# Attention units on one core: the value products issued ahead of the transposes, while score products still come

## The reference, cut to what matters

```python
s = q @ k.T                       # scores; 2nd attention adds a window mask, 4th a position bias
p = softmax(s)                    # 2nd: with one extra "sink" logit in the denominator
o = p @ v
```

## Time and profile before

| | us |
|---|---|
| median of 3 executions | 2563.8 (2560.21 to 2565.89) |
| the profiled execution's own time | 2560.08 |
| span of the profiled execution | 2558.3 |

### The profile page before, as it was taken

How to read it: one execution, slowest core, us unless ns; L and a number is a source line. 1 busy time by engine, 2 the same in 40 slices (tenths; PEclk the granted TensorE clock), 3 DMA queues, 4 the chain that set the end, 5 groups by cost and what they waited for, 6 DMA issues and landing times.

```text
span 2558.3 us, 46168 instructions
## 1 busy us (share of the span) xinstructions
PE 2429.6 (95%) x17946; PEld 1976.9 (77%) x17946; DVE 1678.2 (66%) x2767; ACT 1057.3 (41%) x1748; POOL 375.1 (15%) x340
## 2 busy tenths in 40 slices
PE   7999999989898999999999999889999999899987
PEld 4888888857776788888788888779997875577866
DVE  3777787665555787788877754675555325666665
ACT  4222234365344522222522223555455344555354
POOL 2000011023353200000100001001013700120052
PEclk9999999999999999999999999999999999999999
DMA  7655663200000365566455542324563221023301
GB/s 269 232 192 195 194 204 114 89 23 3 3 4 24 118 208 194 192 195 203 165 195 191 193 142 84 101 75 160 184 175 107 91 95 50 1 66 132 124 18 50
DMA packets 88422, 323.35 MB, mean 126 GB/s; under 512 B 9712, under 2 KB 10864, under 8 KB 87504
## 3 DMA queue, kind: packets, MB, share of 16 engines
q1 hardware_dynamic: 86864, 310.68, 37.3%
q0 software_dynamic: 1408, 10.59, 1.1%
HBM read 320.18 MB, written 1.05 MB: 126 GB/s over the span
## 4 chain that ended last, share of the span: by engine, by line
PE 82%; DVE 9%; ACT 3%; issue 3%; DVEq 1%; DMA 1%; POOL 0%; POOLq 0%; ACTq 0%; SPq 0%
PE bank L503 22%; PE bank L504 22%; PE bank L505 22%; PE bank L1397 1%; DVE row_statistics L1451 1%; PE bank L1406 1%; PE bank L2239 1%; DVE weights_hi_lo L409 1%; PE bank L1422 1%; PE bank L2245 1%; DMA weight_ring<-stream_k 1%; PE bank L1824 1%; ACT weights_hi_lo L404 1%; PE bank L2876 1%; DVE work L3226 1%
## 5 line engine op out<-in xcount | busy, mean ns | idle before, releaser
L404 ACT ACTIVATE weights_hi_lo<-weight_ring 128x1024 fp32r<-128x1024 f32 (+1 forms) x379 | 394.7, 1041 | 1082.3 <-PE bank L505 1057.0
L503 PE MATMUL bank<-input_hi,weights_hi_lo 128*128 128x512 f32 (+1 forms) x2032 | 743.0, 366 | 15.9 <-DVE weights_hi_lo L409 9.8
L409 DVE TENSOR_TENSOR weights_hi_lo<-weight_ring,weights_hi_lo 128x1024 fp32r<-128x1024 f32 (+1 forms) x373 | 453.1, 1215 | 436.9 <-ACT weights_hi_lo L404 435.4
L504 PE MATMUL bank<-input_lo,weights_hi_lo 128*128 128x512 f32 (+1 forms) x2032 | 739.4, 364 | 0.0
L505 PE MATMUL bank<-input_hi,weights_hi_lo 128*128 128x512 f32 (+1 forms) x2032 | 739.4, 364 | 0.0
L503 PEld LDWEIGHTS bank<-input_hi,weights_hi_lo 128*128 128x128 f32 x2032 | 385.7, 190 | 82.9 <-issue 19.8
L504 PEld LDWEIGHTS bank<-input_lo,weights_hi_lo 128*128 128x128 f32 x2032 | 385.7, 190 | 60.5 <-issue 0.7
L505 PEld LDWEIGHTS bank<-input_hi,weights_hi_lo 128*128 128x128 f32 x2032 | 385.4, 190 | 59.7
L503 PE MATMUL bank<-hidden_hi_lo,weights_hi_lo 128*128 128x512 f32 (+1 forms) x936 | 335.6, 359 | 1.4 <-DVE hidden_hi_lo L1111 1.1
L504 PE MATMUL bank<-hidden_hi_lo,weights_hi_lo 128*128 128x512 f32 (+1 forms) x936 | 333.6, 356 | 0.0
L505 PE MATMUL bank<-hidden_hi_lo,weights_hi_lo 128*128 128x512 f32 (+1 forms) x936 | 333.6, 356 | 0.0
(11 more groups left out here) (525 smaller groups left out, 2967.1 us busy)
## 6 DMA issues: line engine op xcount, KB each, us to landing
weight_ring<-stream_k SPq DMA_DIRECT2D x498, 512.0 KB, 3.5
weight_ring<-stream_f SPq DMA_DIRECT2D x64, 448.0 KB, 3.4
weight_ring<-stream_f SPq DMA_DIRECT2D x32, 512.0 KB, 3.7
extra_tiles<-condrows POOLq DMA_DIRECT2D x3, 1024.0 KB, 9.1
constants<-consts POOLq DMA_DIRECT2D x1, 2112.5 KB, 9.4
residual_stream<-xin SPq DMA_DIRECT2D x1, 2048.0 KB, 11.3
work<-nabias POOLq DMA_DIRECT2D x1, 2048.0 KB, 9.4
residual_stream<-ctx POOLq DMA_DIRECT2D x1, 1024.0 KB, 6.0
```

Of the source, the lines that this page charges most:

```text
L404: act.activation(split_place(place)[:, 0, 0:words], w[:, 0:words], ACT.Copy).then_inc(hi_ready, 1)
L409: eng.tensor_tensor(split_place(place)[:, 1, 0:words], ring[:, n % RING, 0:words], split_place(place)[:, 0, 0:words].bitcast(F32), ALU.sub ...
L503: pe.matmul(out, weights[:, 0, w], x_hi, start=first, stop=False)
L504: pe.matmul(out, weights[:, 0, w], x_lo, start=False, stop=False)
```

## The change

In iterations that still issue scores (`it < n`), TensorE multiplies M(it-3) before it transposes T(it-2). In the last three iterations the old order stays. Transposes and value products move unchanged into two helper functions, `turn` and `mix`, with all their waits; instructions, operands and the other engines' programs are the same.

```diff
@@ -1375,6 +1375,34 @@
                 pe.wait_ge(rope_spread, 8)
             if which == "na":
                 pe.wait_ge(heads_ready, a + 1)
+            def turn(u):
+                pe.wait_ge(probs_scaled, u0 + u + 1)
+                if u >= 1:
+                    pe.wait_ge(turned_copied, u0 + u)
+                for b in range(2):
+                    for i in range(len(key_tiles(which, pairs[u][1]))):
+                        mm = pe.transpose(pb[4 + b][:, tok(i)], attention_probs(which, u)[:, b, tok(i)], C("ident"))
+                mm.then_inc(probs_turned, 1)
+
+            def mix(u):
+                t, qt = pairs[u]
+                keys = key_tiles(which, qt)
+                if which == "odd" and u == n - 1:
+                    odd_out_half(pe, 0, range(6))
+                pe.wait_ge(turned_copied, u0 + u + 1)
+                if which == "odd" and u >= 1:
+                    pe.wait_ge(mixed_copied, u0 + u)
+                elif u >= 2:
+                    pe.wait_ge(mixed_copied, u0 + u - 1)
+                for i, tile in enumerate(keys):
+                    for b in range(2):
+                        ch = attention_operands(which, t, b, qt)[2]
+                        mm = pe.matmul(mix_bank(which, u)[HD * b:HD * b + HD, 0:P], attention_values(which, tile, ch),
+                                       attention_turned(which, u)[:, b, tok(i)], start=i == 0, stop=i == len(keys) - 1)
+                mm.then_inc(mixed, 1)
+                if which == "odd" and u == n - 1:
+                    odd_out_half(pe, 1, range(KT - 1))
+
             for it in range(n + 3):
                 if which == "even" and it == 0:
                     pe.wait_ge(qk_normed, 5)
@@ -1396,34 +1424,12 @@
                         q, k, _ = attention_operands(which, t, b, qt)
                         mm = pe.matmul(pb[2 * (it % 2) + b][:, 0:nk], q, k[:, 0:nk], start=True, stop=True)
                     mm.then_inc(scores_ready, 1)
-                u = it - 2
-                if 0 <= u < n:
-                    pe.wait_ge(probs_scaled, u0 + u + 1)
-                    if u >= 1:
-                        pe.wait_ge(turned_copied, u0 + u)
-                    for b in range(2):
-                        for i in range(len(key_tiles(which, pairs[u][1]))):
-                            mm = pe.transpose(pb[4 + b][:, tok(i)], attention_probs(which, u)[:, b, tok(i)], C("ident"))
-                    mm.then_inc(probs_turned, 1)
-                u = it - 3
-                if 0 <= u < n:
-                    t, qt = pairs[u]
-                    keys = key_tiles(which, qt)
-                    if which == "odd" and u == n - 1:
-                        odd_out_half(pe, 0, range(6))
-                    pe.wait_ge(turned_copied, u0 + u + 1)
-                    if which == "odd" and u >= 1:
-                        pe.wait_ge(mixed_copied, u0 + u)
-                    elif u >= 2:
-                        pe.wait_ge(mixed_copied, u0 + u - 1)
-                    for i, tile in enumerate(keys):
-                        for b in range(2):
-                            ch = attention_operands(which, t, b, qt)[2]
-                            mm = pe.matmul(mix_bank(which, u)[HD * b:HD * b + HD, 0:P], attention_values(which, tile, ch),
-                                           attention_turned(which, u)[:, b, tok(i)], start=i == 0, stop=i == len(keys) - 1)
-                    mm.then_inc(mixed, 1)
-                    if which == "odd" and u == n - 1:
-                        odd_out_half(pe, 1, range(KT - 1))
+                if it >= n and it - 2 < n:
+                    turn(it - 2)
+                if 0 <= it - 3 < n:
+                    mix(it - 3)
+                if it < n and it >= 2:
+                    turn(it - 2)
                 yield
 
         def attend_vector(dve, a):
```

## The result

| | before | after |
|---|---|---|
| median, us | 2564.5 (2560.2 to 2565.9, 5 executions) | 2575.2 (2571.9 to 2577.6, 5 executions) |
| profiled execution, its span | 2560.1, 2558.3 | 2571.9, 2570.1 |

The ratio of the two is 1.0045, with a 95% interval from 1.0034 to 1.0056: the changed kernel is slower by 11.5 us (8.7 to 14.4); the two medians of five alone are 10.7 apart. The prediction had 6.9 us and the right sign; the median lies 0.2 us above the range's upper end.

The account below looks back on a forecast made before the run. The prediction took TensorE, busy 95% of the span, as the bound, so reordering could gain only in its idle time. Even 1.6, mla 0.6, na 1.1 and odd 3.6 summed to 6.9 us over 2563.8, giving 2570.7, range 2562.5 to 2575.

Parts of the forecast that it names:

- M is released later than T: All attentions: M waits for its bank's copy, released after T's scale; in even M(9) 0.14 us later than T(10).
- M does fill the holes: Rival, all attentions: M fills about three holes each in even and mla, one each in na and odd; 5.3 us faster, chance 0.09.
- the 62 us: TensorE's idle time before transposes, waiting for VectorE's scale: 34.5 us in even, mla and na, 27.7 in odd.
- the terms of the waits: Delays from M's waits standing ahead of T: even +1.6, mla +0.6, na +1.1, odd +3.6 us.
- Odd's ring: Odd's end: exp, copy, M, T and Tcopy become a closed cycle of 4.0 us per iteration, plus 1.0 for the weight split.
- The 0.4 behind the last slab: Odd: M(7) waits for ScalarE's copy, delaying the next slab product 0.4 us; behind the last slab that stays.
- na, 1.1: Na: T(5) 1.21 us later, exp(7) at 2468.9 instead of 2467.80, carrying the end; +1.1 us, bounds 0 and 2.2.
- The tail that I worked out: Na's end: T(5) 1.21 us later, then Tcopy(5), exp(7) and ScalarE's work to Tcopy(6), +1.1 us.
- M's wait for its own Tcopy comes open: All attentions: M directly behind S exposes its Tcopy wait, which T used to hide; no separate size given.
- takes T's 1.5 us at the low clock: Odd's end: M(10) takes the 1.5 us T had at low clock, so T(11) starts at 1692.8.
- the clock falls more often: Rival, attention starts and odd's end: four more stretches at 1.2 GHz, 1.3 us each, 5.2 more, 2576 us; chance 0.10.
- The delay is taken up: Rival, all attentions: most of exp's lateness vanishes in ScalarE's idle time, leaving 3.4 us, 2567.2, within 0.2%; chance 0.23.

Follow-up runs that it names:

- odd_copy_early: M ahead of T in odd alone, ScalarE copying unit it-3 instead of it-4 at its iteration's head, against the kernel before: ratio 1.0016, +4.1 us.
- odd_slabs: M ahead of T only in odd's iterations before 13, between the weight slabs' products, against the kernel before: ratio 1.0001, no difference told.
- even_only: M ahead of T in the even attention alone, against the kernel before: ratio 1.0006, +1.5 us.
- after_fill: The whole changed kernel plus seven unread identity transposes ahead of the value products in odd's iterations 13 to 15, against the kernel before: 1.0027, +6.9 us.
- na_only: M ahead of T in the na attention alone, against the kernel before: ratio 1.0002, +0.5 us.
- not_odd_copy_early: M ahead of T in even, mla and na, VectorE copying unit it-4 before scaling unit it-1, against the kernel before: 1.0034, +8.7 us.

## Why the prediction was right and wrong

**Right: M is released later than T.** M(9) is named after L1490 and waits 0.48 for L1513 in the next unit; odd's M is named after L1503 in nine waits. With the copy early (odd_copy_early) M starts right behind S. The rival "M does fill the holes" is out: the copy had to come early first to make it true, and without that the kernel is slower.

**Wrong, but without weight in the sum: the 62 us.** They count the weight loads' idle time beside the matmuls'. The matmuls stood 20.6 us for scale; that is all that an M could have filled.

**Right: the terms of the waits.** By the stage lengths with the clock held: even +1.6 (predicted 1.6), mla +0.3 (0.6), odd +3.2 (3.6). Odd's ring is there at 4.04 and 4.05 us per turn (4.0), and at 5.67 with the split (5.0, and 0.67 of it is T at the lower clock, so 5.0 again). The 0.4 behind the last slab is 0.5 in odd_slabs. Inside the terms the agreement is looser, and some of it is luck. In even_only the last four units lose 0.9 (predicted 0.8), the four before them 0.5 (0.8) and the first eight 0.1 (nothing). In odd, behind S(13), 2.5 are lost (3.2), and 0.7 ahead of it (0.4).

**Too small: na, 1.1.** The traces have 1.8 to 2.1. The tail that I worked out is right: T(5) is 1.15 later behind S(7) (1.21 by the prediction), exp(7) 1.05 and Tcopy(6) 1.02 (1.1). What I left out is ScalarE's extra work behind its iteration 4: Tcopy(3) stands behind L3022, and M(3)'s open wait for it, 1.26 us, holds T(4) and S(7), 1.0 more from S(5) to S(7). The step "M's wait for its own Tcopy comes open" says this, and in na it was given no price. The two parts are there in every trace with na's new order: S(5) to S(7) takes 7.8 us (6.8 in the old order), S(7) to the last M 10.1 (9.0). In after_fill and na_only the latter is 11.0, with one more fall of the clock at na's end that no trace with na's old order has.

**Wrong: the clock was priced at nothing in the sum.** The step is "takes T's 1.5 us at the low clock", which assumed that the fall of the earlier trace rows stays where it is, and the rest of the stage at 2.4 GHz. In fact the new holes come one behind the other, 1.09, 1.54, 1.53, 2.47 us, and behind them the clock is at 1.2 GHz for some 10 us instead of for one T, one M and part of an S. Its share is 3.1 us in odd (shown by fillers that take no wait away) and 0.7 in even (53.6 against 52.9, read from traces with and without the fall, not forced). The waits make 1.6 + 0.3 + 2.0 + 3.2 = 7.1 us, so 6.9 was nearly right for them, with luck: na's 0.9 too little and the 0.7 too much in mla and odd cancel. With the clock it is 10.9, and 11.5 was measured. After_fill, with odd's clock held, has 6.9. That is the rival "the clock falls more often", to which I gave 0.10 and 2576 us; it was priced at four stretches of 1.3, 5.2 together, and it came as 3.8 in two places, one of them long.

**"The delay is taken up" is out** for odd by the time, and for even and na by their stages. In even, na and mla the times alone wouldn't refute it.

**What stays open.** In the profiled pair na's start and the stretch from mla's last M to na's first S are together 3.5 us longer than in before, beside the order's 2.0. That is no part of the order in na: seven of the ten traces with the old order in na show the same, and the second of the two lies ahead of na. In all seventeen traces the two go together, a slow start behind the longer stretch (eleven traces) and none behind the shorter (six). What decides which of them an execution gets, and whether the new order in even and odd makes the longer one more frequent, can't be told from one trace for each kernel. Neither can why the clock is lower in not_odd_copy_early.

## What to carry to other kernels

Before moving an instruction into an engine's hole, list every semaphore that it waits for and when each is signalled; the hole is only worth something if all of them are through before the instruction that now ends it. If one isn't, the moved instruction brings its own wait ahead of the one that was there, and if its producer stands behind a consumer of what it now delays, a ring closes whose length can be added up from rows (4.0 predicted, 4.05 found). Then ask what the new idle time does to TensorE's clock: the fall cost as much as the waits, and a few unread transposes in a free bank, fitted inside the hole, tell the two apart. Last, see which engines a sum of idle time counts before taking it for a prize.

## What the runs showed of the hardware

Small unread transposes of the identity kept the granted clock at 1.00 through holes behind which it otherwise fell to 0.50, and so did products; with the transposes the stretch from S(13) to the last M took 21.3 us in place of 24.4.

The clock may fall or not at the same place with the same instructions. At odd's end T(11) waits 1.92 us in before's trace, and the clock falls; it waits 1.94 us in na_only's, with the same order there, and the clock holds. Between mla and na, which no experiment touches, the stretch is 240.6 us long in six traces and 242.2 to 242.3 in eleven, and the windows show the one place where they differ; first before, then the changed kernel at the corresponding place:

```profile
2236.70:2256.70 20.00, 15.15 (x92) 11.81 (x91) 12.75 (x34) 7.53 (x17) 5.99 (x3) 1.00 0.16 53
```

```profile
2243.00:2263.00 20.00, 16.24 (x90) 13.14 (x88) 11.31 (x32) 5.90 (x14) 5.98 (x3) 0.91 0.10 31
```

So a pair of profiled executions can differ by some 3 us where nothing was changed; stage lengths over many traces, held against each other at equal clock, gave terms of a few tenths of a us that the medians could not.

An fp32 product of 128x128 by 128 columns took twice as long as a transpose of that size: 1.83 us for seven (recorded as fourteen) against 0.98 for seven.
